# Laying out a decoder block's inputs on the host: x feature-major, weights tile by tile, parameters as columns

## The reference, cut to what matters

```python
h = rms_norm(x, norm_w)                       # x: (1, 256, 2048)
proj = einsum('btd,de->bte', h, w_in)         # w_in: 2048 x 8204
# columns of proj: 4 retention heads, 6 gated-DeltaNet heads (with a causal conv),
# 12 gate columns (a, b), 6 block-sparse attention heads; each head has 4 x 128 columns
y = concat([y_ret, y_gdn, y_moba])            # each times SiLU of its own gate columns
return x + einsum('bte,ed->btd', y, w_out)    # w_out: 2048 x 2048
```

## Time and profile before

| | |
|---|---|
| median of 3 runs | 510.7 us (510.6 to 510.95) |
| the profiled execution's own time | 510.59 us |
| its span (first to last instruction) | 508.8 us |
| PE, DVE, ACT, POOL busy in the span | 99%, 67%, 55%, 33% |
| DMA | 92.61 MB, 182 GB/s mean |

### The profile page before, as it was taken

One profiled execution on the slowest core, in us unless ns is written; L12 is line 12 of the kernel. 1 busy time (PEld: TensorE's weight loads), 2 busy tenths in 40 slices (PEclk: granted clock), 3 DMA queues, 4 the chain that ended last, 5 costly groups with the idle time before them and its releaser, 6 DMA issues.

```text
span 508.8 us, 8943 instructions
## 1 busy us (share of the span) xinstructions
PE 503.6 (99%) x3442; PEld 424.1 (83%) x3442; DVE 338.8 (67%) x506; ACT 279.0 (55%) x464; POOL 169.8 (33%) x230
## 2 busy tenths in 40 slices
PE   8999999999999999999999999999999999999997
PEld 6888888888888888888888888888888888888885
DVE  5989998889766876564467455755567566646551
ACT  5776756764347676564537354664556456344340
POOL 5763245445122312134054115506050614230000
PEclk9999999999999999999999999999999999999999
DMA  8997666565654556473975676777775557757711
GB/s 280 346 323 200 166 162 169 159 174 144 190 132 122 132 158 158 134 197 69 292 196 145 167 222 164 201 196 190 193 187 168 166 172 232 221 185 222 260 43 41
DMA packets 154988, 92.61 MB, mean 182 GB/s; under 512 B 15971, under 2 KB 143938, under 8 KB 154946
## 3 DMA queue, kind: packets, MB, share of 16 engines
q1 hardware_dynamic: 151456, 89.86, 62.8%
q10 hardware_dynamic: 3490, 2.18, 1.5%
HBM read 89.00 MB, written 2.10 MB: 179 GB/s over the span
## 4 chain that ended last, share of the span: by engine, by line
PE 99%; POOL 0%; DVE 0%; DVEq 0%; issue 0%; POOLq 0%
PE pj L1574 20%; PE pj L1577 20%; PE pj L1576 20%; PE pj L1552 14%; PE pj L1553 7%; PE pj L1630 3%; PE pj L1639 2%; PE mx L1734 1%; PE pj L1549 1%; PE mx L1787 1%; PE mx L1769 1%; PE mx L1601 1%; PE pj L1647 1%; PE mx L1845 1%; PE mx L1907 1%; PE pj L1548 1%
## 5 line engine op out<-in xcount | busy, mean ns | idle before, releaser
L369 DVE TENSOR_TENSOR w_lo<-w_raw,w_hi 128x1024 fp32r<-128x1024 f32 x160 | 200.7, 1262 | 78.2 <-ACT w_hi L489 77.3
L489 ACT ACTIVATE w_hi<-w_raw 128x1024 fp32r<-128x1024 f32 x158 | 166.1, 1057 | 121.0 <-PE pj L1577 103.7
L1574 PE MATMUL pj<-w_hi,hT 128*128 128x512 f32 x320 | 126.5, 395 | 0.0
L1576 PE MATMUL pj<-w_hi,hT 128*128 128x512 f32 x320 | 126.1, 394 | 0.0
L1577 PE MATMUL pj<-w_lo,hT 128*128 128x512 f32 x320 | 124.7, 390 | 0.0
L1552 PE MATMUL pj<-hT,w_hi 128*128 128x512 f32 x300 | 109.0, 403 | 0.0
L1553 PE MATMUL pj<-hT,w_lo 128*128 128x256 f32 x300 | 84.1, 280 | 0.0
L1577 PEld LDWEIGHTS pj<-w_lo,hT 128*128 128x128 f32 x320 | 60.1, 188 | 12.2
L1574 PEld LDWEIGHTS pj<-w_hi,hT 128*128 128x128 f32 x320 | 60.1, 188 | 12.1
L1576 PEld LDWEIGHTS pj<-w_hi,hT 128*128 128x128 f32 x320 | 60.2, 188 | 11.5
L1552 PEld LDWEIGHTS pj<-hT,w_hi 128*128 128x128 f32 x300 | 56.3, 188 | 13.2 <-DVE w_lo L369 0.6
(11 more groups left out here) (239 smaller groups left out, 541.2 us busy)
## 6 DMA issues: line engine op xcount, KB each, us to landing
w_raw<-in_w_in_dram SPq DMA_DIRECT2D x256, 256.0 KB, 3.4
w_raw<-in_w_out_dram SPq DMA_DIRECT2D x64, 256.0 KB, 4.1
big<-in_x_dram SPq DMA_DIRECT2D x9, 256.0 KB, 5.3
out_dram<-sq ACTq DMA_DIRECT2D x7, 256.0 KB, 5.8
big<-in_x_dram SPq DMA_DIRECT2D x3, 512.0 KB, 7.1
cst<-table_dram SPq DMA_DIRECT2D x1, 682.0 KB, 9.3
kq<-vr SPq DMA_DIRECT2D x32, 16.0 KB, 1.8
kq<-mT SPq DMA_DIRECT2D x24, 16.0 KB, 1.9
```

Source lines behind the costliest of these rows:

```text
L369: eng.tensor_tensor(w_lo[:, n % NSPLIT, :], w_raw[:, n % NRAW, :], w_hi[:, n % NSPLIT, :].bitcast(F32), ALU.subtract).then_inc(S("lo"), 1)
L489: act.activation(w_hi[:, n % NSPLIT, :], w_raw[:, n % NRAW, :], ACT.Copy).then_inc(S("hi_done"), 1)
L1574: ins = pe.matmul(bank[:, :], src[:, kc, 0, tok], hi[:, k, :], start=first, stop=False)
L1576: pe.matmul(bank[:, :], src[:, kc, 1, tok], hi[:, k, :], start=False, stop=False)
```

## The change

The host rearranges the inputs before the launch (numpy, outside the time):

- x is also given feature-major (`in_x_turned_dram`). Six pieces of it (256 KiB four times, then 512 KiB twice) go straight into `home`, where POOL's L871 had put whole x. The first stands first on SP's queue. ACT and DVE read it from SBUF, so PE's 32 transposes, `keep_busy` and POOL's 16 additions go.
- The weights lie tile by tile, each partition's 4 KiB in one run. From tile 3 on a tile is one DMA; tiles 0 to 2 are two of 256 KiB (2 KiB runs), and their `w_hi`, `w_lo` and products go by halves (`HALVED`).
- All parameters come as one array of columns, 54 KiB, on ACT's queue; PE's transposes of them and DVE's copies go. The gate weights come in one run of 768 bytes per partition, and POOL multiplies them by `norm_w`, since `home` now holds x without it.
- x's rows (2 MiB, token-major) are loaded as well, in four parts of 512 KiB behind tiles 6, 7 (two) and 8, for the norm alone. ACT alone sums squares, four instructions of 128x1024, two of them after b = 6 and b = 7, one before and one after `w_hi` of tile 8.
- The sums, POOL's power and PE's spreading come later: PE spreads behind `ab_products`, and DVE copies `rb` after that. `w_lo` of tile 8 now comes before `rb`.
- The constant table is split: identity behind tile 5 (68 KiB), what the solve needs behind tile 8 (230 KiB), the rest (452 KiB) behind tile 24, waited for in the retention heads.

```diff
+def weight_tiles(w_in, w_out):
+    tiles = np.empty((TILES, P, TK * 512), np.float32)
...
+        tiles[n] = np.moveaxis(tile, 0, 1).reshape(P, TK * 512)
@@ SyncE
-            load_piece(sp, 0)
             def load(n):
...
+                if n < HALVED:
+                    for k, done in enumerate((f"w_first{n}", f"w_in{n}")):
+                        if n == k == 1:
+                            load_piece(sp, 1)
+                        cols = slice(k * 512, (k + 1) * 512)
+                        sp.dma_start(w_raw[:, n, cols], tiles[n, :, cols]).then_inc(S(done), 16)
+                    return
                 if n >= NRAW:
                     wait_lo(sp, n - NRAW)
...
+                sp.dma_start(w_raw[:, n % NRAW, :], tiles[n]).then_inc(S(f"w_in{n % NRAW}"), 16)
...
+            load_piece(sp, 0)
+            X_AFTER = {1: 2, 2: 3, 3: 4, 5: 5}
+            ROWS_AFTER = {6: (0,), 7: (1, 2), 8: (3,)}
+            SMALL_AFTER, SOLVE_AFTER, LATE_AFTER = 5, 8, 24
@@ ScalarE
-            act.dma_start(cst[:, 0:K_FIRST], table[:, 0:K_FIRST]).then_inc(S("ident_in"), 16)
-            act.dma_start(prow[R_NORM:R_CONV, :], norm_w[0].rearrange("(k p) -> k p", p=P)).then_inc(S("ident_in"), 16)
+            act.dma_start(pcol[:, :], cols).then_inc(S("cols_in"), 16)
...
+            act.wait_ge(S("cols_in"), 16)
+            x_high(1)
             half_high_part(0, 0)
-            act.wait_ge(S("norm_cols"), 1)
-            act.wait_ge(S("hT_psum"), 1)
-            x_high(1)
             half_high_part(0, 1)
-            square_sum(0)
             half_high_part(1, 0)
...
                 if b in SQUARES_AT:
                     square_sum(SQUARES_AT[b])
+            square_sum(2)
+            advance(UPT * (KC // 2 - LEAD + 1))
+            square_sum(3)
             advance(64)
@@ VectorE
+            advance(UPT * (KC // 2 - LEAD) + LOW_AT + 1)
+            total_squares()
+            advance(50)
             dve.wait_ge(S("norm_psum"), 1)
...
             dve.tensor_copy(rb[:, :], mx[1][:, 0:T]).then_inc(S("rb_done"), 1)
-            advance(50)
-            dve.wait_ge(S("norm_psum"), 3)
-            dve.tensor_copy(pcol[:, KC:], mx[2][:, KC:R_ROWS]).then_inc(S("param_cols"), 1)
@@ TensorE
-            all_x_blocks(0)
-            keep_busy(4)
             for t in range(TPH):
...
+                if t < HALVED:
+                    for k in range(TK):
+                        first_group_high(t, (k,))
+                        first_group_low(t, (k,))
+                    continue
+                first_group_high(t, range(TK))
+                first_group_low(t, range(TK))
...
-            pe.wait_ge(S("h_whole"), KC)
+            pe.wait_ge(S("pool_step"), 1)
             ab_products().then_inc(S("abt_psum"), 1)
+            pe.wait_ge(S("pool_step"), 2)
+            for c in range(C):
+                ins = pe.transpose(mx[1][:, c * P:(c + 1) * P], sm[:, 6 + c:7 + c].broadcast_to([P, P]), ident)
+            ins.then_inc(S("norm_psum"), 1)
```

More of the change, by code:

```diff
@@ L133, in constants, with tile_at, section, columns @@
     return t.astype(np.float32)
-def layer(nc, x, norm_w, w_in, conv_w, a_log, dt_bias, ret_norm_w, gdn_norm_w, q_norm_w, k_norm_w, w_out,
-          table, out):
+def tile_at(n):
+    if n < HEADS * TPH:
+        return n // TPH, n % TPH
+    g, q = OUT_TILES[n - HEADS * TPH]
+    return HEADS + g, q
+def section(g, s):
+    return g % 3, s % 2, 2 * (g // 3) + s // 2
+def weight_tiles(w_in, w_out):
+    tiles = np.empty((TILES, P, TK * 512), np.float32)
+    for n in range(TILES):
+        group, q = tile_at(n)
+        rows = slice(q * TK * P, (q + 1) * TK * P)
+        if group >= HEADS:
+            g = group - HEADS
+            tile = w_out[0, rows, g * 512:(g + 1) * 512].reshape(TK, P, 512)
+        elif group == 0:
+            tile = w_in[0, rows, GDN_COL:GDN_COL + 2 * GDN * P].reshape(TK, P, 2, GDN * P)[:, :, :, 0:2 * P]
+        elif group < GDN:
+            p, h, i = section(group, q // 2)
+            at = GDN_COL + (i * GDN + 2 * p + h) * P
+            tile = w_in[0, q % 2 * UPT * P:(q % 2 + 1) * UPT * P, at:at + P].reshape(UPT, P, P)
+        else:
+            kind, j = PAIRS[group // 2]
+            heads, col = {"ret": (RET, RET_COL), "moba": (MOBA, MOBA_COL)}[kind]
+            h = 2 * j + group % 2
+            tile = w_in[0, rows, col:col + 4 * heads * P].reshape(TK, P, 4, heads * P)[:, :, :, h * P:(h + 1) * P]
+        tiles[n] = np.moveaxis(tile, 0, 1).reshape(P, TK * 512)
+    return tiles
+def columns(norm_w, conv_w, a_log, dt_bias, ret_norm_w, gdn_norm_w, q_norm_w, k_norm_w):
+    per_row = [a.reshape(-1, P).T for a in (norm_w, conv_w, ret_norm_w, gdn_norm_w, q_norm_w, k_norm_w)]
+    per_head = [np.broadcast_to(a.reshape(1, GDN), (P, GDN)) for a in (a_log, dt_bias)]
+    return np.ascontiguousarray(np.concatenate(per_row + per_head, axis=1))
+def layer(nc, x, turned_x, tiles, gate_w, cols, table, out):
     ctx = ExitStack()
@@ L552, in square_sum @@
             def square_sum(i):
-                act.wait_ge(S(f"x_in{i + 1}"), X_LANDED[i + 1])
+                c, half = i // 2, slice(i % 2 * D // 2, (i % 2 + 1) * D // 2)
+                act.wait_ge(S(f"rows_in{i}"), 16)
                 if i:
[L556 to L572, removed]
@@ L574, in x_high @@
+                    act.wait_ge(S("squared"), i)
+                act.activation(squares_out, x_rows[:, c, half], ACT.Square, accum_out=sm[:, i:i + 1]).then_inc(S("squared"), 1)
             def x_high(k):
-                act.activation(hT[:, k, 0, :], first_bank(k)[:, k % 2 * T:(k % 2 + 1) * T], ACT.Copy,
+                x_landed(act, k)
+                act.activation(hT[:, k, 0, :], whole(k), ACT.Copy,
                                scale=pcol[:, R_NORM + k:R_NORM + k + 1]).then_inc(S("h_hi"), 1)
+            act.wait_ge(S("cols_in"), 16)
@@ new lines, in _ @@
+            half_low_part(dve, 0, 1)
+            for b in range(1, KC // 2):
+                if b < HALVED:
+                    for k in range(TK):
+                        x_low(2 * b + k)
+                        half_low_part(dve, b, k)
+                    continue
+                x_low(2 * b)
+                x_low(2 * b + 1)
+                advance(UPT * (b - LEAD) + LOW_AT + 1)
+            advance(UPT * (KC // 2 - LEAD) + LOW_AT + 1)
+            total_squares()
+            advance(50)
```

285 lines of the change are left out of this document (104 added, 181 removed).

## The result

The changed kernel takes 511.54 us (median of 22 runs, 510.05 to 512.63) against 510.62 for the kernel before in the same session (22 runs, 510.34 to 511.33): ratio 1.0016, 95% interval 1.0010 to 1.0023. That is 0.9 us slower, inside the band of 0.2% that the prediction called no change; forecast were 508.8 us and a gain, and 511.54 lies above the range (507.0 to 511.0). The scatter grew too, from 1.0 to 2.6 us. Its profiled execution took 511.01 us (span 509.2), faster than most.

The account below looks back on a forecast made before the run. PE's list was taken to bound the kernel until about 34 us, and DVE's list to set tile 16's start. Tile 16 coming 1.8 us earlier gave 510.59 - 1.8 = 508.8 us, range 507.0 to 511.0.

Parts of the forecast that it names:

- First product: Kernel start: less data ahead of the first half tile, landing at 4.4 us, so first product at 5.2 instead of 5.67.
- PE's list up to the gate products: PE before the gate products: list falls from 26.4 us to 22.4 plus 0.25, so they start at 27.9, 4.2 us earlier.
- The first bank: First bank, evacuated behind tile 10's w_hi: ready at 30.8 us, DVE's first addition at 30.9, tile 16 1.8 us earlier.
- DVE after that: DVE from rb to tile 16: 24.9 us list unchanged, so tile 16 moves 2.1 us, not 3.9; rest becomes w_lo waits.
- PE alone decides: Rival, chance 0.13: DVE's list to tile 16 is shorter than read, unit 64's 3.9 us survive less about 0.5: 507.2 us.
- The norm: Norm from x's late rows, ahead of PE's spreading: ready at 29.5 us against PE at 29.8, covered by 0.3 us.
- DMA supply decides: Rival, chance 0.25: tile 10 and x's last rows land late; no gain at 382 GB/s, slower kernel below it.
- The clock falls: Rival, chance 0.04: PE idle from 4.2 to about 5.2 us drops to half rate; tile 0 costs 2.8 us: 511.6.
- At nothing: Items priced at zero: fewer issues, 4 KiB runs, late table part, POOL's early instructions, DVE reading x, everything behind tile 16.
- it doesn't arrive: Rival, chance 0.04: the gain is swallowed further on by a wait that now has slack: 510.6 us.

Follow-up runs that it names:

- g3: Changed kernel with three more warm-up products and 17 small ones behind the norm's spreading (80 more instructions in all): 510.71 us, ratio 0.9996 to the kernel before.
- i1: Changed kernel with two more warm-up products and 18 small ones behind the norm's spreading: 510.98 us, ratio 1.0001 to the kernel before.
- i3: h3 again, unchanged, on the same chip as its parts: 509.93 us, ratio 0.9984 to the kernel before.
- i2: i1 with FIRST_EV = 1, so VectorE adds one bank instead of two at the start: 510.85 us, ratio 1.0001 to the kernel before.
- e1: Changed kernel, but ScalarE evacuates the first two banks ahead of w_hi of tile 10 instead of behind it: 511.62 us, ratio 1.0016 to the kernel before.
- e3: Changed kernel with FIRST_EV = 1, moving the second bank's addition and scaling from VectorE to GpSimd: 511.60 us, ratio 1.0015 to the kernel before.
- g2: Changed kernel with 20 products of 32 by 32 on TensorE behind the norm's spreading (80 more instructions): 511.16 us, ratio 1.0002 to the kernel before.
- i4: Changed kernel again, unchanged, on the same chip as its repaired versions: 512.14 us, ratio 1.0023 to the kernel before.
- e2: Changed kernel without the four loads of x's rows, squaring feature-major x instead (norm not the reference's): 511.61 us, ratio 1.0012 to the kernel before.
- h4: Changed kernel with the weights from tile 24 on in four DMAs of 1 KiB runs instead of one of 4 KiB runs: 511.38 us, ratio 1.0010.
- e4: Kernel before with FIRST_EV = 1, taking the second bank's addition and scaling off VectorE's list: 510.62 us, ratio 0.9997 to the kernel before.
- g4: Kernel before with only the weights laid out tile by tile, one 512 KiB DMA with 4 KiB runs per tile: 513.53 us, ratio 1.0047.
- h1: Kernel before with 43 products of 32 by 32 on TensorE before 1.3 us, one warm-up product less: 515.49 us, ratio 1.0081 to the kernel before.
- g1: Changed kernel with three more warm-up products of 256 columns behind its two: 511.48 us, ratio 1.0015 to the kernel before.
- h2: Changed kernel without the loads of x's rows, with two more warm-up products and 18 small ones behind the spreading: 509.50 us, ratio 0.9969.
- h3: Changed kernel with more warm-up and small filler products, first two banks evacuated ahead of tile 10's split, one bank for VectorE: 509.59 us, ratio 0.9975.

## Why the prediction was wrong

**First product: size off.** Forecast 5.2, bounds 4.8 to 5.6; it came at 5.62. The half tile landed at 4.9, not 4.4. The columns' DMA in 428-byte runs moved beside it and needed until 4.43; that it was the reason is not shown.

**PE's list up to the gate products: size off by as much.** 28.80 less 5.62 is 23.2 us against 22.65 forecast; together the gate products came 0.9 us later than the 27.9 of the text. With 0.4 us of waiting for the norm this put `rb` at 31.14, and the first addition behind it at about 31.6 instead of 30.6: 0.7 of the 1.8 us were lost before the bank comes in.

**The first bank: this step took what was left of the forecast gain.** Tile 10 was to land at 29.0 and landed at 30.95. The rate was forecast well (412 to 420 GB/s; 413 to 421 from 12 us on). Part of the miss is the start: 273 and 296 GB/s from 2 to 8 us are about 1.5 MB between 3 and 8 us, 0.6 less than at 412, so 1.4 us where the text gave 0.8. That makes 29.6. The other 1.3 us are in the landing itself: 10.42 MB, all that stood up to tile 10, had moved by 29.2 us, and by 30.95 some 11.2 MB had, so packets of later tiles moved ahead of tile 10's last. Tile 9 was as late: it landed at 29.7, and ACT was at its split until 30.8, so a prompt landing of tile 10 alone would have given only 0.17 us. The start of tile 10's split varied from 30.2 to 31.5 us over the profiles (g3, i1). i3 against i2 bears the step out: with the first banks ahead of tile 10's split the median is 0.9 us lower. It is then 1.1 us below the kernel before, with all repairs and one bank, and still 0.7 short of the forecast gain.

**DVE after that: right.** No pause between the first addition and `w_lo` of tile 16, and PE's waits for `w_lo` between 31 and 58 us grew from 0.3 to 1.6 us, as forecast (1.5 to 2.5). So the rival *PE alone decides* falls.

**The norm: not covered.** It was to be ready 0.3 us ahead of PE. Squares were done at 29.1 and POOL's result came at 30.3, so PE waited 0.4 us for it; the bank came later still and hid this wait.

***DMA supply decides***, the second rival, is what happened in kind, but not by its number: the rate was above its point of 382 GB/s, and the landing still came at 30.95. The Trainium skill, "DMA: Bandwidth & Descriptors", section "Where 436 GB/s comes from", would have read 358; the 415 measured here disagree, as the earlier trace rows did.

***The clock falls***, chance 0.04: no fall is in any trace, but the slow first products that this rival priced are there. Seven profiles are of changed kernels that leave PE idle from 4.2 to about 5.6 us; in four of them (e1, e3, g2, i4; not in the first profile, e2 and h4) the first products ran at half pace for 3 to 5 us. What they show is a late rise. In all seven the warm-up's load at 3.18 us takes 0.34 us (0.33 in two), as at the lower level of 1.2 GHz, and the trace's own record of the full level (2.4 GHz) begins at 4.3 to 4.4 us in the three and at 9.1, 9.3, 10.2 and 10.8 in the four; the lower level comes back only after the last product. Where PE had large products almost without a break from 1.3 us on, the record begins at 4.6 to 6.4 us (before, e4, g4) and at 4.8 to 7.3 (the seven with longer warm-ups); in h1, whose 43 small products fill PE from 0.9 to 5.7 us, at 10.7. So a longer warm-up shortens the slow stretch and does not always end it: i3's first eight products still took 1.86 us. The granted clock reads 1.00 in both windows of i4 above, because this view counts the time ahead of the first record as full: durations had to be read, not that column. The Trainium skill, "TensorE: Matmul & The Clock Gate", Part 1, calls the lower level the default, which activity lifts; these rows agree, and the fall of an idle PE that the prediction took from there is shown by none.

With the late rise PE reaches the gate products at 29.9 to 30.5 instead of 28.6 to 28.8, so the loss is 1.1 to 2.0 us there; the prediction had 2.8. Part of it was masked, since DVE waited for the bank in any case: at 111 us i4 is 0.06 us behind the changed kernel's first profile, e1 and g2 are 0.5 and 0.7 behind.

***"Behind tile 16 nothing changes"*, a sentence of the step *At nothing*, is the step that failed.** It put at nothing all that comes behind, and there the changed kernel lost about 0.9 us. The step was meant of work and queues, and it missed that deleting 38 products and their loads in front shifts every later block of instructions. In the kernel before a block ends 2.8 us ahead of the solve's first burst, and the block that PE enters there lasts 6.5 us; in the changed one the ends lie inside the first, second and third burst, at 123.84, 127.97 and 132.41. Added up over the eight bursts, the seven profiles with the changed kernel's blocks (after, e1, e2, e3, g1, h4, i4) have 0.3 to 1.6 us of stops, 0.9 on average. Of ten with the blocks of the kernel before (before, e4, g2, g3, g4, h2, h3, i1, i2, i3) seven have under 0.1 us, g4 0.2, i3 0.24 and h3 1.1.

The ends alone do not make a stop: from the second burst on they lie inside bursts in the kernel before too (127.42, 131.81 and so on), 4.1 to 4.4 us apart in both. What differs is when the packet for the third burst starts: 1.5 to 3.7 us after PE entered the second burst's new block in the seven, and from 1.6 us ahead of that to 1.9 us after it in the ten. So the longer block ahead of the first burst goes with earlier fetches; why they start when they do is not shown.

The stops and the longer wait for `w_lo` ahead of the first burst account for the loss from 111 to 153 us: that of e2 is 1.8 us, with 1.5 of stops and 0.24 of the wait; that of e3, with one bank, 1.05, with 1.0 of stops; that of the changed kernel's first profile 0.47, with 0.29 and 0.24.

The rival *it doesn't arrive* named the pattern (a gain swallowed further on) but for a wait that has slack; it was no such wait.

The sum as it should have been, from these profiles: a gain at tile 16 of 0.05 instead of 1.8, a wait of 0.24 ahead of the first burst, and stops of 0.9 on average, with what the half pace leaves in some executions. From the 510.62 us of the kernel before in the same session that gives about 511.7, an estimate; measured were 511.54. Two errors of one sign add up in it: a gain that did not come, and a loss that was put at nothing.

## What to carry to other kernels

Removing instructions from a saturated engine moves the ends of its instruction blocks everywhere behind the edit: look for equal small instructions that pause "for issue" at one product, and move the ends by filling an idle stretch with a few that do nothing. When warm-up work is removed, keep the engine busy up to the first real product, and judge its pace by durations: the best version still had some slow first products. And when a transfer lies ahead of a result in another engine's order, take the result out from behind it before counting on the transfer's rate.

## What the runs showed of the hardware

- PE's instructions come in packets of 16 KB, 256 instructions each by the distance of two stops (e2). A packet took 0.9 to 1.3 us mostly (up to 2.3), PE could go on 1.3 to 1.6 us after its end, and beside weight traffic it started up to 4.0 us (h3) after PE had entered the block before. The Trainium skill, "Runtime: NRT & Kernel Launch", section "Instruction fetch mechanics", gives the same blocks and calls crossing one mostly hidden. Between tiles' large products that held; in bursts of small ones, where PE needs a block every 4.1 to 4.4 us, it did not always (stops of 0.3 to 1.6 us in seven of seven profiles with one position of the blocks, of 0.2 to 1.1 us in three of ten with the other).
- A DMA queue of tiny packets (0.21 MB in 2322) slowed when the other queue's packets grew, in the one case run: 96 KiB of gate weights landed after 21.1 us beside 4 KiB runs and after 12.4 beside the kernel before's (g4).
- TensorE's clock rose to its full level between 4.3 and 10.8 us after the start; with PE idle from 4.2 to 5.6 us it was 9.1 us or later in four of seven profiles, with PE kept busy by large products never later than 7.3 in ten; h1, with small ones, 10.7.
- One record of a 32 by 32 product took 56 ns at the cold start (h1), 11 in the solve's bursts and 37 behind the spreading (g3, 34 in 1.26 us).
